# Moving two of the four PSUM copies of each attention step from ScalarE to VectorE, and the weight split ahead of the copies

## The reference

```python
parts = jnp.split(h @ w_in[l], split_points, axis=-1)     # q, six k/v, gates, sgu, s5, 3 x 1024 branch gates
y_a = nsa_attention(...) @ w_attn_o[l]                    # compressed, selected and window branch
y_b = spatial_gating(...) @ w_sgu_o[l]
y_c = s5_layer(...) @ w_s5_o[l]
g_a, g_b, g_c = jnp.split(jax.nn.sigmoid(branch_g), 3, axis=-1)
x = x + (g_a * y_a + g_b * y_b + g_c * y_c) @ w_mix_o[l]
x = x + hierarchical_moe(rms_norm(x, norm_ffn_g[l]), ...)
```

## Time and profile before

| | |
|---|---|
| time of the profiled execution | 2035.84 us |
| its span, first to last instruction | 2034.2 us |
| median of three runs | 2035.84 us |
| PE, PEld, DVE, ACT, POOL busy | 1955.2, 1116.1, 930.8, 400.9, 7.5 us |
| mean granted TensorE clock | 0.977 |
| attention loop, either layer | 178 us long |

### The profile page before, as it was taken

The page is one execution under the profiler, slowest core; times in us unless marked ns, Lnnn a source line. Parts: engine busy times, 40 slices in busy tenths (PEclk is TensorE's granted clock), DMA queues, the critical chain, the costliest instruction groups (busy, mean ns, idle before and its releaser), DMA issues. The chain is left out here.

```text
span 2034.2 us, 25488 instructions
## 1 busy us (share of the span) xinstructions
PE 1955.2 (96%) x9936; PEld 1116.1 (55%) x9937; DVE 930.8 (46%) x1935; ACT 400.9 (20%) x814; POOL 7.5 (0%) x25
## 2 busy tenths in 40 slices
PE   6999999999899999999879999999998999999996
PEld 3458777644644544554434687776454544554542
DVE  7743555342534333443478245553333434433434
ACT  3204444201211111101221044441021111101112
POOL 0000000000000000000000000000000000000000
PEclk9999999999799999999989999999998999999998
DMA  6111111412599999999641012123325999999994
GB/s 246 47 58 63 63 63 56 153 69 104 224 428 428 427 426 427 423 429 421 290 148 47 21 63 83 48 78 124 160 93 233 426 428 423 429 427 424 422 429 172
DMA packets 45259, 484.16 MB, mean 238 GB/s; under 512 B 9456, under 2 KB 9968, under 8 KB 15472
## 3 DMA queue, kind: packets, MB, share of 16 engines
q1 hardware_dynamic: 45168, 482.90, 58.1%
HBM read 476.59 MB, written 6.29 MB: 237 GB/s over the span
## 5 line engine op out<-in xcount | busy, mean ns | idle before, releaser
L1651 DVE TENSOR_TENSOR x_tokens<-x_tokens,ps 128x512 f32<-128x512 f32 x240 | 161.7, 687 | 236.0 <-PE ps L897 234.8
L963 PE MATMUL ps<-arena,branch 128*64 128x512 f32 x512 | 226.6, 595 | 0.0
L963 PE MATMUL ps<-slabs,branch 128*64 128x512 f32 x512 | 226.6, 595 | 0.0
L914 PE MATMUL ps<-arena 128*64 128x512 f32 x512 | 225.1, 592 | 0.0
L913 PE MATMUL ps<-arena 128*64 128x512 f32 x512 | 225.1, 592 | 0.0
L914 PE MATMUL ps<-slabs,arena 128*64 128x512 f32 x512 | 225.0, 592 | 0.0
L913 PE MATMUL ps<-slabs,arena 128*64 128x512 f32 x512 | 224.9, 592 | 0.0
L723 PE MATMUL ps<-h_hi,w_parts 128*128 128x512 f32 x768 | 211.8, 411 | 0.0
L723 PEld LDWEIGHTS ps<-h_hi,w_parts 128*128 128x128 f32 x768 | 139.1, 192 | 36.5 <-issue 10.1
L559 PE MATMUL ps<-slabs,hT 128*128 128x512 f32 x320 | 142.1, 604 | 9.2 <-DVE hT L1246 9.1
L913 PEld LDWEIGHTS ps<-slabs,arena 128*64 128x64 f32 x512 | 70.1, 137 | 146.2 <-issue 146.2
(11 more groups left out here) (333 smaller groups left out, 2733.4 us busy)
## 6 DMA issues: line engine op xcount, KB each, us to landing
arena<-in_expert_w_gate SPq DMA_DIRECT2D x32, 2048.0 KB, 12.0
arena<-in_expert_w_up SPq DMA_DIRECT2D x32, 2048.0 KB, 16.5
arena<-in_expert_w_down SPq DMA_DIRECT2D x32, 2048.0 KB, 9.3
slabs<-in_expert_w_gate SPq DMA_DIRECT2D x32, 2048.0 KB, 15.0
slabs<-in_expert_w_up SPq DMA_DIRECT2D x32, 2048.0 KB, 19.5
slabs<-in_expert_w_down SPq DMA_DIRECT2D x32, 2048.0 KB, 13.8
slabs<-in_dense SPq DMA_DIRECT2D x16, 2048.0 KB, 7.9
slabs<-in_gate_w SPq DMA_DIRECT2D x24, 1024.0 KB, 4.8
```

The costliest lines, as they stand in the source:

```text
L914: return nc.tensor.matmul(ps[64:P, BANK_GU[b], :], xk, high[:, k, :], start=(k == 0), stop=(k == ND - 1), tile_position=(0, 64))
L963: done = nc.tensor.matmul(ps[64 * b:64 * b + 64, BANK_Y[half], :], hidT[:, k, CAP * b:CAP * (b + 1)], w_down[b][:, k, half * 512:(half + 1 ...
L1651: v.tensor_tensor(xs, xs, ps[:, BANK_BACK[n % 2], :], ALU.add).then_inc(s["back_added"], 1)
```

## The change

ScalarE's `turned` and its four uses go away, and with them the `gate` call that stood ahead of them. VectorE makes all four copies of a step: units 0 and 1 where it made them, units 2 and 3 after `weighted(i)`. `split_lo` moves from the end of VectorE's step to the place behind `masked(i)`, ahead of `outputs` and the copies. The number of pieces in each step stays as it was. TensorE's list is the same.

```diff
--- before.py
+++ after.py
@@ -1110,14 +1110,6 @@
                     nc.scalar.activation(c_scf, c_scf, ACT.Exp).then_inc(s["cexp_done"], 1)
                     before = sum(FILL)
                     gate(before // GATE_MM)
-
-                    def turned(i, j):
-                        n = (i // R + 1) * P
-                        act.wait_ge(s["tr_done"], 4 * i + j + 1)
-                        if i >= 1:
-                            act.wait_ge(s["pv_done"], i)
-                        nc.scalar.activation(probT[j][:, 0:n], ps[:, BANK_TURN, 0:n], ACT.Identity).then_inc(s["pt_evac"], 1)
-
                     for i in range(N_ATT):
                         n = (i // R + 1) * P
                         for j in range(4):
@@ -1125,14 +1117,7 @@
                             p = prob[i % 2][:, j, 0:n]
                             nc.scalar.activation(p, p, ACT.Exp, scale=-1.0, bias=negmax[:, 4 * (i % 2) + j:4 * (i % 2) + j + 1],
                                                  accum_out=rowsum[:, 4 * i + j:4 * i + j + 1]).then_inc(s["exp_done"], 1)
-                        begun = before + sum(sum(FILL_STEP[u // R]) for u in range(i)) + FILL_STEP[i // R][0]
-                        gate(begun // GATE_MM)
-                        if i >= 1:
-                            turned(i - 1, 2)
-                            turned(i - 1, 3)
                         gate((before + sum(sum(FILL_STEP[u // R]) for u in range(i + 1))) // GATE_MM)
-                    turned(N_ATT - 1, 2)
-                    turned(N_ATT - 1, 3)
                     gate(24)
 
                     for m, (kind, t, half) in enumerate(TAIL):
@@ -1549,6 +1534,10 @@
                     for i in range(N_ATT + 1):
                         if i < N_ATT:
                             masked(i)
+                        if i >= 1:
+                            due = LO_PIECES * (filled // (2 * GATE_MM) + 2) - lows[0]
+                            split_lo(due)
+                        filled += sum(FILL_STEP[i // R] if i < N_ATT else LAST_FILL)
                         if i >= R + 1 and (i - 1) % R == 0:
                             outputs((i - 1) // R - 1)
                         if i >= 1:
@@ -1557,8 +1546,8 @@
                         if i < N_ATT:
                             weighted(i)
                         if i >= 1:
-                            split_lo(LO_PIECES * (filled // (2 * GATE_MM) + 2) - lows[0])
-                        filled += sum(FILL_STEP[i // R] if i < N_ATT else LAST_FILL)
+                            turned(i - 1, 2)
+                            turned(i - 1, 3)
                     outputs(NT - 1)
 
                     dve.wait_ge(s["proj_free"], J_GATE + 24)
```

## The result

| | before | after |
|---|---|---|
| median, us (lowest to highest) | 2035.63 (2034.87 to 2040.01), 4 runs | 2067.73 (2066.41 to 2069.47), 4 runs |
| profiled execution, span, us | 2035.84, 2034.2 | 2065.34, 2063.6 |
| granted clock, mean | 0.977 | 0.980 |
| loop: start of the first `scores` to start of the last `values`, us, layer 0 / 1 | 172.82 / 172.90 | 188.25 / 188.25 |

The change makes the kernel slower, by a ratio of 1.0158 (95% interval 1.0139 to 1.0178). The forecast was 2064 us and the range 2053 to 2074. The medians differ by 32.1 us; in the two profiled executions the loops grew by 30.8 us together and the span by 29.4.

The account below looks back on a forecast made before the run. The prediction took TensorE as the bound, with copy-to-transpose margins in the attention stage deciding: 9.1 + 4.9 + 0.1 = 14.1 us a layer, 28 us in two, on 2035.8 gives 2064 us; range 2053 to 2074.

Parts of the forecast that it names:

- What bounds: Attention stage: when each copy is done against TensorE's next transposes decides, not busy sums; step 14 margins 0.5 and 0.38 us.
- Part 1: Split ahead of the first copy delays the second transposes in nine steps, 9.1 us a layer; high part costs no wait.
- Part 2: Third copy, queued behind `weighted` on VectorE, delays the fourth transposes: 4.9 us a layer, mostly in steps 12 to 15.
- Part 3: Fourth copy, now on VectorE, delays `values` only in step 16, which has no fill there: 0.1 us a layer.
- The release: Restart of TensorE's transposes after a wait for VectorE's copy: 0.11 us each, taken from one earlier wait.
- The rival with a costlier release: Each of 24 waits a layer costs 0.24 us to restart, not 0.11: 2070 us, chance 0.15.
- The sum: Both attention stages together: 14.1 us a layer, 28 us in two, giving 2064 us, 1.4% slower.
- the sign of being wrong: Any stage outside attention changing by over 1 us would show the forecast wrong.
- Work: Busy time over the kernel: VectorE some 31 us more, ScalarE 28 us less, from 64 moved copies.
- Only the split costs: Rival: the third copy behind `weighted` is never waited for, only the split ahead of copies costs: 2054 us, chance 0.13.
- Not slower: Rival: ScalarE's relief at each loop's end decides, - 1.4 us in all, 2034 us; chance 0.07.
- The clock falls: Rival: stalls lower TensorE's clock once in steps 13, 14, 15 of each layer, 20 us on top, 2084 us; chance 0.05.

Follow-up runs that it names:

- Experiment 3: Changed kernel with all four VectorE copies right behind mask and outputs, then the weighting, split last: 2036.08 us, ratio 1.0002 to the kernel before.
- experiment 2: Kernel before with only the split moved behind the mask, ahead of outputs and copies; copies 2 and 3 stay on ScalarE: 2054.98 us, ratio 1.009.
- Experiment 1: Changed kernel with the split put back to the very end of VectorE's step: 2048.95 us, ratio 1.0064 to the kernel before.
- experiment 5: Changed kernel with the split left behind the weighting, ahead of the third copy: 2107.14 us, ratio 1.034 to the kernel before.

## Why the prediction was right, step by step

**What bounds.** That the margins between copy and transposes decide, and not the sums of work, was right. Experiment 3 shows it most directly: the same sums, and no loss.

**Part 1, forecast 9.1 us a layer.** Measured 9.25, and alone, in experiment 2, 9.6 with what follows the releases. The nine steps came out within 0.04 us each. That the split does not wait for the high part was right too: in step 14 its pieces start right at the end of the mask.

**Part 2, forecast 4.9 us a layer.** Measured 5.3. The shape was right (nothing much up to step 7, then 0.30, 0.45, 0.72, 0.87), but the values lie up to 0.05 us above their forecasts and the small steps sum to 0.33 where I had 0.14.

**Part 3, forecast 0.1 us a layer.** Measured 0.10.

**The release, forecast 0.11 us each.** This is the term that was too small. After a copy of VectorE ends, the weight load starts 0.12 us later and the matmuls 0.15 us later, and the group takes 0.63 us in place of 0.60 (step 13 after, fourth transposes: the copy ends at 362.68):

```profile
362.80 0.42 PEld L785 LDWEIGHTS ps<-arena 128*128 128x128 f32 x4 [1.11 <-DVE xn_tokens L1518]
362.83 0.63 PE L785 MATMUL ps<-arena 128*128 128x128 f32 x4 [0.71 <-DVE branch L1525]
```

That is 0.18 us and not 0.11. With 17 such places in a layer (9 + 8) the 0.07 us make 1.2 us, and the whole shortfall is 15.4 - 14.1 = 1.3 us. The match is a rough one: by stretches the 1.3 us are 0.15 us in part 1, 0.4 us in part 2 and 0.8 us in the stretches right behind a release, to which the forecast gave nothing, and some 0.4 us of it lies in steps 1 to 7, around fourth transposes for which no wait is listed. The rival with a costlier release put 0.24 us on it: the truth lies between the two, and the time, 2067.7 us, lies between 2064 and 2070. In the one row from which I took it, the wait was for an add of VectorE, and TensorE started 0.05 us behind its end; ahead of these transposes it is 0.15, and that in each of the 34 stops of the two loops (0.145 to 0.147). It is not the copy: in step 16 the same copy releases `values` at 403.76, 0.06 us behind its end. The transposes have two waits in the program ahead of them (p_ready and pt_evac) and `values` of step 16 has one (pt_evac); whether that makes the difference, no run tests.

**The sum.** 28 us were forecast, the loops grew by 30.8, the span by 29.4 and the median by 32.1. Outside the loops the profiled execution was 1.4 us shorter. The two windows between and behind the loops have a clock of 0.98 where they had 0.97. Against it, one wait of TensorE in the router was 8.1 us in place of 5.9. Experiment 1 has the 8.1 us too and experiments 2 and 3 have 5.9, so it does not go with the split or with the copies; I put both down to differences from run to run, and have not shown it. Over the nine profiles here the stretch between the two loops took 829.5 to 837.1 us (833.7 before, 833.0 after) and the one behind them 638.6 to 641.4 us. So the sign of being wrong that the forecast set at 1 us outside the stage was narrower than these stretches repeat.

**Work.** VectorE was to be busy for 31 us more and has 27.4, ScalarE for 28 less and has 25.6. Both terms were too large, in part since two instructions of VectorE in a row overlap by 0.08 us and busy time counts the overlap once. No time hangs on them.

**The rivals.** "Only the split costs" fell: experiment 1 has 16 waits and 12 us without it. "Not slower" fell with the first wait of step 14. "The clock falls" did not occur in the change and did in experiment 5; the stalls were up to 1.5 us long here and 2.3 to 3.1 us there. No loop of these runs has stalls between these. Its price of 3.4 us a fall was an upper bound: the 11 falls of experiment 5 cost some 1.5 us each (below). What the prediction tells of frequent short idles stands in the same page of the Trainium skill, but in the section behind the one that it names (A second HAM failure mode: psum-queue depth-cycling); the change, with its short waits and a clock of 1.00 in both loops, does not show it.

## What to carry to other kernels

When two engines hand one buffer back and forth, busy sums say nothing: for each handover write down when the consumer arrives and when the producer is done, and hold each added instruction against that margin. In these loops what stayed under it was free and what exceeded it cost its full length, plus about 0.2 us for the stop. On the engine that owes the handover, put the copies first and the work that nobody waits for last: here the same instructions cost the two loops 0.3 us in one order, 31 us in another and 72 us in a third.

## What had not been expected of the hardware

A stop of TensorE costs more than its recorded idle time. In step 14 the record shows 0.87 us of idle, while the transposes start 1.03 us later than without the wait. The rows of the fill ahead of them, before and after, hold the difference:

```profile
359.58 0.62 PE L723 MATMUL ps<-h_lo,w_parts 128*128 128x512 f32 x2
...
372.36 0.62 PE L723 MATMUL ps<-h_lo,w_parts 128*128 128x512 f32 x2
```

Before, the fill ended at 360.20 and the transposes had begun at 360.04, an overlap of 0.16 us; after, they begin 0.87 us behind its end (372.98 to 373.85), and the overlap is gone too. Over both loops the recorded waits ahead of transposes sum to 22.7 us and the loops are 30.8 us longer. Who reads only the list of waits sees three quarters of the loss.

Stalls that are long enough cost twice. In experiment 5, 53.9 us of late fourth transposes (26.9 and 27.0) were joined by 18.0 us elsewhere in the loops (9.8 and 8.2). Experiment 1, whose fourth transposes wait in 16 places with no fall of the clock, has 1.0 us elsewhere in its two loops, so some 17 us go with the 11 falls, about 1.5 us each. A stall of the same length need not bring a fall: step 1 has the same stall in both layers (2.31 and 2.33 us), and the clock fell behind the one of layer 0 alone.
